# Gated heads: the place of one weight tile's rounding, and where the next stage's first products stand on TensorE

## The chip, the cores and the metric

One core of one Trainium2 chip runs the whole program. The metric is device time in microseconds (us), from runs of the kernel before and of the changed one. PE is TensorE (matrix products), PEld its weight loads, DVE is VectorE, ACT is ScalarE, POOL is GpSimd, and SP is SyncE, which here only issues DMAs.

## What is computed

The program computes two blocks of a network over 768 tokens (256 of context and 512 of a grid) with a width of 1024. The change touches one stage of the second block: the eight gated heads. Cut to what matters:

```python
f, k = lb + (1 - lb) * sigmoid(f_raw), 1 - f        # both directions
gcum = cumsum(log f) within a chunk of 128 tokens
att  = einsum('bhtd,bhtsd,bhsd->bhts', q, exp(gcum_t - gcum_s), k)
o    = einsum('bhts,bhsv->bhtv', att, v) + einsum('bhtd,bhdv->bhtv', q * exp(gcum), s)
s    = exp(glast) * s + einsum('bhsd,bhsv->bhdv', k * exp(glast - gcum), v)
o    = rms_norm(o_forward + o_backward) * silu(gate)
```

Here `f_raw` (for the forward and the backward direction), `q`, `v` and `gate` are projections of the tokens with columns of the matrix `w_in`. The stage after it, the grouped state-space stage, needs `dt`, a further 64 columns of `w_in`, and projections of its own.

## The kernel before

**Projections.** `gated_heads` walks over 41 weight tiles: for each head h five of them, FF and FB (`f_raw` of the two directions), Q, V and G (the gate), in this order, and then one tile for `dt`. A weight tile is 128 x 1024 in float32. It arrives by a DMA from SP into one of two slots of `ring`. ACT rounds it to its high part (`high(n)`, a CAST, L3119), DVE subtracts to get the low part (`low(n)`, L3273), both into `ring_twin`, and SP loads the tile after the next into the slot once the low part is made. PE then makes three products for each of eight slices of the width: L366, L367 and L368, in `product3`. Eight slices make a lot: 24 matmuls of 128 x 384 for half of all tokens (FF, FB and V have two lots each), or 24 of 128 x 512 for the grid's tokens alone (Q and G). One slice of a lot, three matmuls, is a unit here. Lots go by turns into banks 6 and 7 of PSUM, and ACT copies each out (`evict`, L3125).

**A head.** The order on each engine is written out by hand. Every head runs through 14 places, `at` = 1 to 14. On PE, `fill(FILL[at - 1])` puts so many units of the projection behind the head's own work at each place, 64 units or eight lots in all. The projection runs nine lots ahead of the head: during head h PE projects the second half of FF of head h + 1 up to the first half of FF of head h + 2. That last lot begins in the fill of place 12 and is the first to use the tile `n + 5 + FF`. In the last head only one lot, eight units, is left, and it is used up at places 1 and 2.

**Levels.** The decays between two tokens of a chunk are made on seven levels. For each, POOL takes differences of cumulated logs (L2970, L2971, into `hg_dec`, two buffers), ACT exponentiates (`near`, L3194), DVE multiplies by keys and queries (`mixed`, L3317 and L3318, into `hg_mix`), PE multiplies (`products(lv)`, L3039), and DVE puts the result into `hg_att` (`kept`, L3327 and L3330). Products of levels 0 to 7 stand at the head's start and at places 1 to 7. Beside them stand the transposes of v (L3074, place 1), of the weighted keys (`key_rows`, L3054, places 2 and 5), the state updates (`updates`, L3064, places 3 and 6; DVE's `states`, L3339) and at place 10 the head's output (L3090, L3093), eight matmuls of attention and sixteen of states in the trace's count of two passes each.

**The end of a head.** ACT makes the decays of the next head at place 12 (`decays`, L3155 to L3159, for the directions 0 and 1), which DVE weights by the keys at place 13 (`weighted`, L3307 and L3309), and DVE makes the next head's first `mixed` at place 14. DVE's `pre` (L3350) and `tail` (L3356), PE's `squares` (L3045) and ACT's `rstd` (L3169, L3170) normalise a head's output.

**The last head and the next stage.** `leading()` makes the next stage's first two lots (16 units) inside this one, with `lead(count)`; they stay in banks 6 and 7, and the next stage copies them out. In the last head `dt` is transposed through PSUM at place 7 (L3100) and copied out by ACT (L3232, `dt_kept`), and DVE and ACT work on it at places 9 to 11. A stage ends with a barrier of all engines; the next stage's first evictions are L3702.

Of the kernel before, what the change touches and what calls it, by code (L numbers as in the profile page):

```python
# [14 lines left out]
P = 128  # L15
# [4 lines left out]
NC = T // P  # L20
# [2868 lines left out]
def gated_heads(core, k, hT, lower, norm_w, oT, dt, loga, par, ready, base, onward):  # L2889
# [4 lines left out]
    nc, d, ps = core.nc, core.dram, k.ps  # L2894
    H, LV, DEC = HG_HEADS, LEVELS, 2
    PART = (((0, 384), (384, 384)), ((NCTX, NX),))
    with ExitStack() as ctx:
# [16 lines left out]
        dT, dT2, dt_tmp = v[0:64, :], f[0:64, 0, :], f[:, 1, 0:64 * NC].rearrange("p (c a) -> p c a", c=NC)  # L2914
        dt_rows, loga_rows = (a.rearrange("p c a h -> p c (a h)") for a in (dt, loga))
# [8 lines left out]
        FF, FB, Q, V, G = range(5)  # L2924
# [16 lines left out]
        with core.stage("w_in*2", "const_in", "high_ready", "low_ready", "lot_done", "evicted", "sig_ready", "f_ready",  # L2941
# [38 lines left out]
            def _(pe):  # L2980
# [21 lines left out]
                def leading():  # L3002

                    for a, (n, t0, nt) in enumerate(((0, 0, 384), (0, 384, 384))):
                        at = ring_at(len(tiles) + n)
                        pe.wait_ge(low_ready, len(tiles) + n + 1)
                        pe.wait_ge(evicted, len(lots) - 1 + a)
                        if a == 0:
                            pe.wait_ge(dt_kept, 1)
                        for j in range(KD):  # L3010
                            c = slice(P * j, P * j + P)
                            mm = product3(pe, ps[:, 6 + a, 0:nt], (wh[:, at, c], wl[:, at, c]),
                                          (hT[0][:, j, t0:t0 + nt], hT[1][:, j, t0:t0 + nt]), j == 0, j == KD - 1)
                            if j == KD - 1:
                                mm.then_inc(lot_done, 1)
                            yield
                leads = leading()

                def lead(count):
                    for _ in range(count):  # L3020
                        next(leads, None)

                fill(72)
                for h in range(H):
                    p = h % 2

                    def products(lv):
                        a = att_of(h, lv)
                        if a >= 2:
                            pe.wait_ge(att_kept, a - 1)  # L3030
                        if lv == 0:
                            pe.wait_ge(q_ready, h + 1)
                        else:
                            pe.wait_ge(mix_ready, level_of(h, lv))
                        for c in range(NXC):
                            t = slice(P * c, P * c + P)
                            keys, queries = (ks[:, t], q[:, p, t]) if lv == 0 else (mix[:, level_of(h, lv) % 2, 0, t],
                                                                                 mix[:, level_of(h, lv) % 2, 1, t])
                            mm = pe.matmul(ps[:, a % 2, t], keys, queries, start=True, stop=True)  # L3039
                        mm.then_inc(att_done, 1)  # L3040

                    def squares(h):
                        pe.wait_ge(sq_ready, h + 1)
                        pe.wait_ge(pre_ready, h + 1)
                        pe.matmul(ps[:, 5, :], k.ones[:], scr[:], start=True, stop=True).then_inc(ss_done, 1)  # L3045
# [20 lines left out]

                    products(0)
                    for at in range(1, 2 * LV + 1):
                        if at <= LV:
                            products(at)  # L3070
                        if at == 1:
                            pe.wait_ge(evicted, lot_of(h, V, 1) + 1)
                            for c in range(NC):
                                mm = pe.transpose(turn(c), v[:, P * c:P * c + P], k.ident[:])  # L3074
                                if c in (3, NC - 1):
                                    mm.then_inc(vt_done, 1)
                        if at == 2:
                            key_rows(0)
                        if at == 3:
                            updates(0)  # L3080
                        if at == 5:
                            key_rows(1)
                        if at == 6:
                            updates(1)
                        if at == 10:
                            pe.wait_ge(att_kept, (h + 1) * (LV + 1))
                            pe.wait_ge(S_ready, 2 * h + 2)
                            for c in range(NXC):
                                o = ps[:, 5, P * c:P * c + P]
                                pe.matmul(o, vt[:, C0 + c, :], att[:, c, :], start=True, stop=False)  # L3090
                                for dr in range(2):
                                    slot = ORDER[dr][C0:].index(C0 + c)
                                    mm = pe.matmul(o, S[:, dr, slot, :], qe[:, p, dr, P * c:P * c + P], start=False, stop=(dr == 1))  # L3093
                            mm.then_inc(o_done, 1)
                        if at == 2 and h > 0:
                            squares(h - 1)
                        if at == 7 and h + 1 == H:
                            pe.wait_ge(dt_turned, 2)
                            for c in range(NC):
                                mm = pe.transpose(ps[:, 6, 64 * c:64 * c + 64], dT2[:, P * c:P * c + P], k.ident[0:64, 0:64])  # L3100
                            mm.then_inc(dt_done, 1)
                        fill(FILL[at - 1])
                        if h + 1 == H and at > 8:
                            lead((3, 3, 3, 3, 2, 2)[at - 9])
                squares(H - 1)

            @block.scalar
            def _(act):
# [88 lines left out]
                for h in range(H):  # L3197
                    m, n, last = 8 * (h + 1), 5 * (h + 1), h + 1 == H
                    for at in range(1, 2 * LV + 1):
# [29 lines left out]
                        if at == 8:  # L3229
                            if last:  # L3230
                                act.wait_ge(dt_done, 1)
                                act.copy(dt_rows, ps[:, 6, 0:64 * NC].rearrange("p (c a) -> p c a", c=NC)).then_inc(dt_kept, 1)  # L3232
                            act.preload_act_table_set("sigmoid_and_others")
                            if not last:
                                forget(h + 1)
# [17 lines left out]
                            squares(h)  # L3253
                        if at == 12 and not last:
                            decays(h + 1, 0)
                            decays(h + 1, 1)
                            evict(m + 6)
                        if at == 13 and not last:
                            high(n + 5 + FF)
                            near(h + 1, 1)  # L3260
                rstd(H - 1)

# [1 line left out]
            def _(dve):  # L3264
# [105 lines left out]
                for h in range(H):  # L3370
                    n, last = 5 * (h + 1), h + 1 == H
                    for at in range(1, 2 * LV + 1):
# [41 lines left out]
                        if at == 12:  # L3414
                            pre(h)
                        if at == 13 and not last:
                            weighted(h + 1, 0)
                            low(n + 5 + FF)
                        if at == 14 and not last:
                            mixed(h + 1, 1)  # L3420
                        if at == 5 and h > 0:
# [773 lines left out]
```

## Time and profile before

| | |
|---|---|
| time of the kernel, median of 3 | 3500.74 us (3500.51 to 3502.58) |
| the profiled execution | 3506.6 us, span 3504.8 us |
| PE busy | 3281.6 us, 94% |
| DVE busy | 2541.5 us, 73% |
| ACT busy | 1616.3 us, 46% |
| POOL busy | 546.7 us, 16% |
| granted clock of PE, mean | 0.969 |

The gated heads' stage runs from about 846 us to 1324 us of the span. The profiler's execution is one of its own; its rows add up to 3504.8 us, and a difference made from them is carried over to the median. The granted clock of PE has two levels, 2.4 GHz (1.0 in the rows) and 1.2 GHz (0.5); a stretch with a value between them has some of each.

### The profile page before, as it was taken

The numbers are of one execution on the slowest core, as the hardware profiler recorded it, in microseconds if no ns is written. First come the engines' busy times: TensorE is split into PE (matmuls) and PEld (weight loads), VectorE is DVE, ScalarE is ACT, GpSimd is POOL, SyncE is SP. The second block draws the span as 40 slices with busy tenths as digits, with TensorE's granted clock in tenths as the row PEclk, the third lists the DMA queues.
The fourth block names the chain that finished last, engine by engine and source line by source line (L and its number), as shares of the span: only waits on it lengthen the run. The fifth ranks groups of instructions, "written<-read, shape, count | busy, mean of one in ns | idle before, by whom it ended". The sixth has DMA issues, their size and how long they took to land. (4 is left out here: it accounts for less than half of the span.)

```text
span 3504.8 us, 48242 instructions
## 1 busy us (share of the span) xinstructions
PE 3281.6 (94%) x18404; PEld 2863.2 (82%) x18404; DVE 2541.5 (73%) x4368; ACT 1616.3 (46%) x2671; POOL 546.7 (16%) x357
## 2 busy tenths in 40 slices
PE   7997998997999999999998997999997999999997
PEld 3886997775898888888876885999886888999996
DVE  2656886254788786888884444899995887888886
ACT  4433432324555554676664323333663444444444
POOL 0211000000324330000000000455000111222220
PEclk9998999998999999999999999999998999999999
DMA  5101110342111102111113234344468998999994
GB/s 218 44 25 55 31 37 19 114 175 90 49 49 49 49 31 62 55 55 61 55 55 131 91 139 175 117 144 141 156 216 305 352 356 332 351 358 350 347 358 151
DMA packets 152468, 521.20 MB, mean 149 GB/s; under 512 B 19136, under 2 KB 66096, under 8 KB 132400
## 3 DMA queue, kind: packets, MB, share of 16 engines
q1 hardware_dynamic: 133808, 383.90, 30.9%
q0 software_dynamic: 18432, 134.23, 10.2%
q8 instruction: 147, 2.41, 0.3%
q14 instruction: 81, 0.66, 0.1%
HBM read 474.01 MB, written 44.06 MB: 148 GB/s over the span
## 5 line engine op out<-in xcount | busy, mean ns | idle before, releaser
L366 PE MATMUL ps<-hT_high,ring_twin 128*128 128x384 f32 (+1 forms) x1768 | 691.2, 391 | 55.6 <-DVE ring_twin L3273 33.1
L368 PE MATMUL ps<-hT_high,ring_twin 128*128 128x384 f32 (+1 forms) x1768 | 646.2, 366 | 0.0
L367 PE MATMUL ps<-hT_low,ring_twin 128*128 128x384 f32 (+1 forms) x1696 | 617.9, 364 | 0.0
L366 PEld LDWEIGHTS ps<-hT_high,ring_twin 128*128 128x128 f32 x1768 | 341.5, 193 | 106.4 <-DVE ring_twin L3273 38.6
L368 PEld LDWEIGHTS ps<-hT_high,ring_twin 128*128 128x128 f32 x1768 | 340.1, 192 | 31.5
L367 PEld LDWEIGHTS ps<-hT_low,ring_twin 128*128 128x128 f32 x1696 | 328.4, 194 | 30.1 <-issue 4.3
L366 PE MATMUL ps<-ex_vh,ex_al 128*128 128x512 f32 x768 | 301.0, 392 | 21.7 <-DVE ex_al L2812 21.7
L2331 POOL TENSOR_TENSOR pr_wl<-pr_w,pr_wh 128x1024 fp32r<-128x1024 f32 x58 | 147.1, 2538 | 1005.3 <-ACT pr_wh L2390 1005.3
L368 PE MATMUL ps<-ex_vh,ex_ah 128*128 128x512 f32 x768 | 301.5, 393 | 0.0
L367 PE MATMUL ps<-ex_vl,ex_ah 128*128 128x512 f32 x768 | 301.4, 392 | 0.0
L2667 POOL DMA_INDIRECT ex_uv<-in_peer_uv,rows_at x128 | 168.6, 1317 | 810.8 <-DVE ex_acc L2771 570.6
L2722 ACT CAST ex_vh<-ex_v 128x1024 fp32r<-128x1024 f32 x128 | 134.1, 1048 | 163.8 <-PE ps L368 135.3
L2807 DVE TENSOR_TENSOR ex_vl<-ex_v,ex_vh 128x1024 fp32r<-128x1024 f32 x128 | 156.4, 1222 | 54.8 <-ACT ex_vh L2722 54.8
L366 PEld LDWEIGHTS ps<-ex_vh,ex_al 128*128 128x128 f32 x768 | 145.3, 189 | 52.4 <-DVE ex_vl L2807 16.4
L368 PE MATMUL ps<-ex_xh,ex_uh 128*128 128x384 f32 x512 | 171.9, 336 | 0.0
L366 PE MATMUL ps<-ex_xh,ex_ul 128*128 128x384 f32 x512 | 171.7, 335 | 0.0
L367 PE MATMUL ps<-ex_xl,ex_uh 128*128 128x384 f32 x512 | 171.5, 335 | 0.0
L368 PEld LDWEIGHTS ps<-ex_vh,ex_ah 128*128 128x128 f32 x768 | 145.0, 189 | 30.5
L367 PEld LDWEIGHTS ps<-ex_vl,ex_ah 128*128 128x128 f32 x768 | 145.2, 189 | 29.1
L2771 DVE SCALAR_TENSOR_TENSOR ex_acc<-ex_uv,ex_wts,ex_acc 128x1024 f32<-128x1024 f32 x127 | 162.6, 1280 | 4.1 <-DVE ex_acc L2771 0.5
L366 PE MATMUL ps<-ex_xh,pr_wl 128*128 128x384 f32 (+1 forms) x464 | 162.9, 351 | 1.1 <-POOL pr_wl L2331 1.1
L368 PE MATMUL ps<-ex_xh,pr_wh 128*128 128x384 f32 (+1 forms) x464 | 162.3, 350 | 0.0
(610 smaller groups left out, 7604.4 us busy)
## 6 DMA issues: line engine op xcount, KB each, us to landing
ex_v<-in_peer_uv SPq DMA_DIRECT2D x128, 512.0 KB, 7.0
pr_w<-in_peer_u SPq DMA_DIRECT2D x64, 512.0 KB, 3.8
ex_u<-in_peer_u SPq DMA_DIRECT2D x64, 512.0 KB, 7.9
ring<-in_w_in_ma SPq DMA_DIRECT2D x48, 512.0 KB, 3.3
gates_by_expert<-sg_gbuf SPq DMA_DIRECT2D x6, 4096.0 KB, 15.0
ex_g<-gates_by_expert SPq DMA_DIRECT2D x32, 768.0 KB, 8.2
ring<-in_w_in_hg SPq DMA_DIRECT2D x40, 512.0 KB, 3.3
ring<-in_w_merge SPq DMA_DIRECT2D x36, 512.0 KB, 3.7
```

The lines of the kernel that those rows point to most:

```text
L366: pe.matmul(out, a[1], b[0], start=start, stop=False)
L367: pe.matmul(out, a[0], b[1], start=False, stop=False)
L368: return pe.matmul(out, a[0], b[0], start=False, stop=stop)
L2331: pool.tensor_tensor(wl[:, n % R, :], w[:, n % W, :], wh[:, n % R, :].bitcast(F32), ALU.subtract).then_inc(low_ready, 1)
L2667: pool.indirect_dma_start(uv[:, n % UV, :], None, d["peer_uv"], bass.IndirectOffsetOnAxis(ap=rows_at[:, n:n + 1], axis=0)).then_inc(uv_in[ ...
L2722: act.copy(vh[:, m % R, :], v[:, m % R, :]).then_inc(vh_ready, 1)
L2771: dve.scalar_tensor_tensor(out=acc[:], in0=uv[:, n % UV, D:2 * D], scalar=wts[:, n:n + 1], in1=acc[:], op0=ALU.mult, op1=ALU.add).then_inc ...
L2807: dve.tensor_tensor(vl[:, m % R, :], v[:, m % R, :], vh[:, m % R, :].bitcast(F32), ALU.subtract).then_inc(vl_ready, 1)
```

## The change

It has four parts. First, in heads 0 to 6, the CAST of the tile `n + 5 + FF` on ACT moves from the start of place 13 to place 12, between the decays of the two directions, and its subtraction on DVE moves at place 13 ahead of `weighted(h + 1, 0)`. Second, on PE the transposes of v at place 1 move ahead of `products(1)`, in all heads. Third, the `dt` transposes go to bank 5 in place of bank 6 and wait for `rstd` of the head before, so that the leading lots no longer wait for `dt_kept`; the last head's output at place 10, which also uses bank 5, waits for it instead. Fourth, the 16 units of `lead` move from places 9 to 14 (3, 3, 3, 3, 2, 2) to places 3 to 10 (2, 1, 2, 1, 2, 1, 1, 3), with the last 3 behind the last `squares`.

```diff
@@ leading
                         pe.wait_ge(evicted, len(lots) - 1 + a)
-                        if a == 0:
-                            pe.wait_ge(dt_kept, 1)
@@ tensor
                     for at in range(1, 2 * LV + 1):
-                        if at <= LV:
-                            products(at)
                         if at == 1:
                             pe.wait_ge(evicted, lot_of(h, V, 1) + 1)
                             for c in range(NC):
                                 mm = pe.transpose(turn(c), v[:, P * c:P * c + P], k.ident[:])
                                 if c in (3, NC - 1):
                                     mm.then_inc(vt_done, 1)
+                        if at <= LV:
+                            products(at)
...
                         if at == 10:
                             pe.wait_ge(att_kept, (h + 1) * (LV + 1))
                             pe.wait_ge(S_ready, 2 * h + 2)
+                            if h + 1 == H:
+                                pe.wait_ge(dt_kept, 1)
...
                         if at == 7 and h + 1 == H:
                             pe.wait_ge(dt_turned, 2)
+                            pe.wait_ge(rstd_ready, h)
                             for c in range(NC):
-                                mm = pe.transpose(ps[:, 6, 64 * c:64 * c + 64], dT2[:, P * c:P * c + P], k.ident[0:64, 0:64])
+                                mm = pe.transpose(ps[:, 5, 64 * c:64 * c + 64], dT2[:, P * c:P * c + P], k.ident[0:64, 0:64])
                             mm.then_inc(dt_done, 1)
                         fill(FILL[at - 1])
-                        if h + 1 == H and at > 8:
-                            lead((3, 3, 3, 3, 2, 2)[at - 9])
+                        if h + 1 == H:
+                            lead((0, 0, 2, 1, 2, 1, 2, 1, 1, 3, 0, 0, 0, 0)[at - 1])
                 squares(H - 1)
+                lead(3)
@@ scalar
-                                act.copy(dt_rows, ps[:, 6, 0:64 * NC].rearrange("p (c a) -> p c a", c=NC)).then_inc(dt_kept, 1)
+                                act.copy(dt_rows, ps[:, 5, 0:64 * NC].rearrange("p (c a) -> p c a", c=NC)).then_inc(dt_kept, 1)
...
                         if at == 12 and not last:
                             decays(h + 1, 0)
+                            high(n + 5 + FF)
                             decays(h + 1, 1)
                             evict(m + 6)
                         if at == 13 and not last:
-                            high(n + 5 + FF)
                             near(h + 1, 1)
@@ vector
                         if at == 13 and not last:
+                            low(n + 5 + FF)
                             weighted(h + 1, 0)
-                            low(n + 5 + FF)
```

ACT's order from the first decays to the first level's exponential, in the first full head before the change (the CAST of `ring` is `high`):

```order
L3155 ACTIVATE hg_ebl<-hg_cum 128x6
L3157 ACTIVATE hg_qe<-hg_cum 128x512
L3159 ACTIVATE hg_kd<-hg_kd 128x768
L3125 COPY hg_v<-ps 128x384
L3119 CAST ring_twin_50<-ring 128x1024
L3194 ACTIVATE hg_dec<-hg_dec 128x1024 x2
```

And the same stretch of ACT after the change, from the last instruction of the first direction's decays on:

```order
L3161 ACTIVATE hg_kd<-hg_kd 128x768
L3121 CAST ring_twin_50<-ring 128x1024
L3157 ACTIVATE hg_ebl<-hg_cum 128x6
L3159 ACTIVATE hg_qe<-hg_cum 128x512
L3161 ACTIVATE hg_kd<-hg_kd 128x768
L3127 COPY hg_v<-ps 128x384
L3196 ACTIVATE hg_dec<-hg_dec 128x1024 x2
```

The CAST has moved past three activations and one copy; nothing else of ACT's order changes in these heads.

DVE's order at the same place before the change, from the head's `pre` (`oT`) to the next head's first `mixed`:

```order
L3350 SCALAR_TENSOR_TENSOR oT<-ps,hg_norm_w,hg_gate 128x512
L3307 TENSOR_TENSOR hg_kd<-hg_kd,hg_k 128x768
L3309 TENSOR_TENSOR hg_qe<-hg_qe,hg_q 128x512
L3273 TENSOR_TENSOR ring_twin_50<-ring,ring_twin_50 128x1024
L3317 TENSOR_TENSOR hg_mix<-hg_dec,hg_k 128x512
L3318 TENSOR_TENSOR hg_mix<-hg_dec,hg_q 128x512
```

DVE's order there after the change:

```order
L3352 SCALAR_TENSOR_TENSOR oT<-ps,hg_norm_w,hg_gate 128x512
L3275 TENSOR_TENSOR ring_twin_50<-ring,ring_twin_50 128x1024
L3309 TENSOR_TENSOR hg_kd<-hg_kd,hg_k 128x768
L3311 TENSOR_TENSOR hg_qe<-hg_qe,hg_q 128x512
L3319 TENSOR_TENSOR hg_mix<-hg_dec,hg_k 128x512
L3320 TENSOR_TENSOR hg_mix<-hg_dec,hg_q 128x512
```

The subtraction stands two instructions earlier; what comes before and behind the three is the same.

PE's order in the last head before the change, from the products of level 3 to the first leading unit (L366; `hg_f` is `dt` here):

```order
L3039 MATMUL ps<-hg_mix 128x128 x4
L3064 MATMUL ps<-hg_vt,hg_ktok 128x128 x5
L3039 MATMUL ps<-hg_mix 128x128 x8
L3054 MATMUL ps<-ident,hg_kd 128x128 x6
L3039 MATMUL ps<-hg_mix 128x128 x4
L3064 MATMUL ps<-hg_vt,hg_ktok 128x128 x5
L3039 MATMUL ps<-hg_mix 128x128 x4
L3100 MATMUL ps<-ident,hg_f 128x64 x6
L366 MATMUL ps<-hT_high,ring_twin_50 128x384
```

PE's order there after the change, from the end of the unit before level 4 to the first unit behind the second transposes of keys:

```order
L368 MATMUL ps<-hT_high,ring_twin_50 128x384
L3037 MATMUL ps<-hg_mix 128x128 x4
L366 MATMUL ps<-hT_high,ring_twin_50 128x384
L367 MATMUL ps<-hT_low,ring_twin_50 128x384
L368 MATMUL ps<-hT_high,ring_twin_50 128x384
L3037 MATMUL ps<-hg_mix 128x128 x4
L3052 MATMUL ps<-ident,hg_kd 128x128 x6
L366 MATMUL ps<-hT_high,ring_twin_50 128x384
```

Levels 4 and 5, which stood back to back (x8), now have a leading unit between them, and each later place has one or two, up to place 10.

## Rows read from the trace of the kernel before

**Rows 1.** The page: PE's busy time (us, share of the span, instructions).

```profile
PE 3281.6 (94%) x18404; PEld 2863.2 (82%) x18404; DVE 2541.5 (73%) x4368; ACT 1616.3 (46%) x2671; POOL 546.7 (16%) x357
```

**Rows 2.** PE's waits, 940 to 1290 us: total us, times, longest us.

```profile
PE ps L366 <- DVE ring_twin L3273: 15.2, 7, 2.2
```

**Rows 3.** Windows from wait to wait: stretch, us, each engine's busy us, PE clock.

```profile
1002.53:1057.59 55.06, 52.90 (x321) 49.91 (x321) 43.86 (x57) 31.09 (x44) 19.56 (x15) 0.97 0.15 49
1112.63:1166.11 53.48, 51.33 (x321) 48.34 (x321) 43.87 (x57) 31.08 (x44) 19.57 (x15) 1.00 0.15 50
```

**Rows 4.** Timeline of PE up to one such wait: start us, us, instruction, [idle before].

```profile
994.72 0.39 PE L366 MATMUL ps<-hT_high,ring_twin 128*128 128x512 f32 x1
...
999.97 0.39 PE L368 MATMUL ps<-hT_high,ring_twin 128*128 128x512 f32 x1
1002.53 0.44 PE L366 MATMUL ps<-hT_high,ring_twin 128*128 128x384 f32 x1 [2.17 <-DVE ring_twin L3273]
```

**Rows 5.** Timeline of DVE, 996 to 1010 us.

```profile
997.81 1.19 DVE L3307 TENSOR_TENSOR hg_kd<-hg_kd,hg_k 128x768 f32<-128x768 f32 x1
998.92 1.57 DVE L3309 TENSOR_TENSOR hg_qe<-hg_qe,hg_q 128x512 f32<-128x512 f32 x1
1000.42 2.06 DVE L3273 TENSOR_TENSOR ring_twin<-ring,ring_twin 128x1024 fp32r<-128x1024 f32 x1
...
1004.00 0.68 DVE L3318 TENSOR_TENSOR hg_mix<-hg_dec,hg_q 128x512 f32<-128x512 f32 x1
```

**Rows 6.** Timeline of ACT, 993 to 1005 us.

```profile
994.60 0.85 ACT L3159 ACTIVATE hg_kd<-hg_kd 128x768 f32<-128x768 f32 x1 [0.26 <-DVE hg_kd L3300]
...
997.26 0.85 ACT L3159 ACTIVATE hg_kd<-hg_kd 128x768 f32<-128x768 f32 x1 [0.26 <-DVE hg_kd L3300]
...
998.38 1.05 ACT L3119 CAST ring_twin<-ring 128x1024 fp32r<-128x1024 f32 x1
```

**Rows 7.** Timeline of SP, 975 to 1000 us.

```profile
983.57 8.69 SPq L2958 DMA_DIRECT2D ring<-in_w_in_hg  x2
```

**Rows 8.** The page: DMA issues by line, KB each, us to landing.

```profile
ring<-in_w_in_hg SPq DMA_DIRECT2D x40, 512.0 KB, 3.3
```

**Rows 9.** Timeline of DVE ahead of head 0, 889.5 to 899 us.

```profile
890.53 2.11 DVE L3273 TENSOR_TENSOR ring_twin<-ring,ring_twin 128x1024 fp32r<-128x1024 f32 x1
892.56 1.84 DVE L3307 TENSOR_TENSOR hg_kd<-hg_kd,hg_k 128x768 f32<-128x768 f32 x1
...
897.37 0.68 DVE L3318 TENSOR_TENSOR hg_mix<-hg_dec,hg_q 128x512 f32<-128x512 f32 x1
```

**Rows 10.** Timeline of PE at the start of the next head.

```profile
1008.39 1.05 PE L3039 MATMUL ps<-hg_q,hg_sg 128*128 128x128 f32 x8
...
1010.17 0.82 PE L3074 MATMUL ps<-ident,hg_v 128*128 128x128 f32 x6
1010.74 0.42 PE L366 MATMUL ps<-hT_high,ring_twin 128*128 128x384 f32 x1
```

**Rows 11.** PE's waits, 1290 to 1330 us, the last head and behind it.

```profile
PE ps L3039 <- DVE hg_mix L3318: 5.8, 3, 2.4
PE ps L366 <- ACT ma_raw L3702: 4.3, 1, 4.3
```

**Rows 12.** Windows over the last head's middle and the next stage's first lot.

```profile
1293.20:1310.00 16.80, 10.36 (x58) 9.56 (x58) 14.76 (x26) 6.38 (x9) 5.13 (x4) 0.70 0.00 1
...
1325.87:1332.60 6.73, 6.73 (x27) 6.73 (x27) 0.60 (x7) 1.29 (x2) 0.00 (x0) 0.63 0.65 164
```

**Rows 13.** Timeline of PE, end of the last head.

```profile
1313.69 0.42 PE L366 MATMUL ps<-hT_high,ring_twin 128*128 128x384 f32 x1
...
1320.54 1.02 PE L3045 MATMUL ps<-hg_scr,ones 128*128 128x512 f32 x2
```

**Rows 14.** Timeline of DVE, end of the last head.

```profile
1314.82 0.74 DVE L3350 SCALAR_TENSOR_TENSOR oT<-ps,hg_norm_w,hg_gate 128x512 f32<-128x512 f32 x1
1322.98 0.69 DVE L3356 TENSOR_TENSOR oT<-oT,hg_scr 128x512 f32<-128x512 f32 x1 [7.42 <-ACT hg_scr L3170]
```

## Prediction

> **What bounds the kernel now.** I began with the page: PE is busy for 94% of the span [rows 1], so in this stage a gain must come from PE's own idle time or from its clock. Next I asked who PE waits for in the heads. From 940 to 1290 us there is one line only: seven waits, 15.2 us together, all for DVE's low part of a weight tile [rows 2]. They are the seven uses of the tile `n + 5 + FF`, one in each of heads 0 to 6. Then I cut the stage from one wait to the next. A head takes 55.06 us at a mean clock of 0.97, but one of them, which has the same wait and as many instructions, takes 53.48 us at 1.00 [rows 3]. So a wait costs twice: PE stands for 2.17 us, and in six of the seven heads the clock goes to its lower level for a moment behind it, which costs 55.06 - 53.48 = 1.58 us more.
>
> The timelines say why the tile is late. PE issues its last product of lot G at 999.97 and is free for the next about 0.23 us later (products of 512 columns follow each other at that distance), at 1000.2. It starts at 1002.53 [rows 4], right behind the end of the subtraction, 1000.42 + 2.06 = 1002.48 [rows 5]. DVE has by then done two operations that nobody needs before the next head. ACT's CAST runs from 998.38 to 999.43 [rows 6], so in the old order not even ACT was early enough: both halves of the move are needed.
>
> **Part 1, the tile's rounding.** *ACT.* The first direction's decays end at 994.60 + 0.85 = 995.45, and the second's last activation starts at 997.26, when DVE releases it [rows 6]. Between stand two short activations (0.8 us in all), which fit behind a CAST from 995.45 to 996.50: they end at 997.3. So the 1.05 us go into time in which ACT waited, and the second decays are late by 0.05 us or nothing. The CAST itself needs two things. Its slot must be free, which is so when the last lot of V is done, at 994.7, where lot G starts [rows 4]. Its data must have landed: issued at 983.57 [rows 7], plus 3.3 us [rows 8], is 987. Neither makes it wait. *DVE.* The subtraction now starts where `weighted` started, 997.81 [rows 5], 1.3 us after the CAST. It takes 2.06 us there and 2.11 us at most [rows 5, 9], POOL being at work beside it each time, so it is done by 999.92, and PE wants it at 1000.2. The margin is 0.3 us by the worst row and 1.2 us if it took only what `weighted`'s first operation took there, 1.19 us. I take the wait as wholly gone: 15.2 us.
>
> The Trainium skill bears on this margin ("SBUF — State Buffer", section "SBUF: two separate sides"): VectorE with two SBUF inputs and GpSimd share a port pair that is locked for a whole instruction, and the loser blocks. The rows agree so far that the same subtraction takes 2.06 to 2.11 us beside POOL. By the rule DVE would lose at most the rest of one POOL instruction, so the sum would be the same, and only the chance of a late tile smaller.
>
> *The clock.* With the wait gone I expect the lower clock behind it gone too: 6 x 1.58 = 9.5 us. The trace's one head at 1.00 shows that it is no fixed part of a head; it does not show that the waits cause it, since that head had its wait as well. The Trainium skill ("TensorE: Matmul & The Clock Gate", section "HAM oscillation") puts the loss at the throttled time multiplied by one half. With the clock of 0.97 in 55.06 us the shortfall is 1.65 us a head and the sum 9.9 us instead of 9.5 us, which changes nothing that I conclude.
>
> *What is late next.* PE arrives at the next head 2.17 + 1.58 = 3.75 us earlier against DVE, so 1008.39 becomes 1004.6 [rows 10]. `products(0)` reads old data. `products(1)` needs DVE's `mixed`, which ended at 1004.00 + 0.68 = 1004.68 [rows 5]; in the new order the same five operations run in the same stretch. The opening, ahead of head 0, already has the new order there: 890.53 to 898.05, 7.52 us [rows 9], against 997.81 to 1004.68, 6.87 us. So `mixed` ends between 1004.7 and 1005.3.
>
> **Part 2, transposes first.** Products 0 and 1 take 1010.17 - 1008.39 = 1.78 us together, 0.89 us each, and the transposes 1010.74 - 1010.17 = 0.57 us [rows 10]. `products(1)` would be due at 1004.6 + 0.9 = 1005.5 in the old order, 0.2 us behind the worst case, and 1006.1 in the new. It moves no work and is worth nothing by itself; it makes the cover thicker. ACT gets v's transposes 0.9 us earlier, DVE the products of level 1 0.6 us later, and neither was waited for by PE. The sum of part 1 is 15.2 + 9.5 = 24.7 us.
>
> **Parts 3 and 4, the last head.** Here PE has no projection left behind place 2 and waits three times for `mixed`, 5.8 us [rows 11], with a clock of 0.70 in the 16.8 us around it [rows 12]: 0.30 x 16.8 = 5 us of full speed are missing there. A unit is (1320.54 - 1313.69) / 13 = 0.53 us [rows 13]. Ten units stand now at places 3 to 9, 5.3 us, almost the size of the waits that they fill. Some of them sit in front of `products` or `updates` and would delay the chain that DVE walks, yet PE works more evenly, which should give back part of the clock. Most of what the clock costs there lies in or beside waits, so I count an eighth to a half of the 5 us for the moment at which the head's output can start, 0.6 to 2.5 us, and take 1.5 us. The bound on the bad side is 5.3 us later, if no unit fell into a wait.
>
> Behind the output there were 13 units, from 1313.69 to 1320.54, and only then `squares`, `rstd` and `tail` (to 1322.98 + 0.69 = 1323.67 [rows 14]). `pre`, which `squares` needs, had long been ready. Now three units end at 1315.3 by that clock, and `squares` starts at 1314.82 + 0.74 = 1315.56 rather than 1320.54: 5.0 us less. The `dt` work on ACT and DVE that stands ahead of `pre` doesn't start earlier than the output does, so I take 4.6; at the lower clock three units take 3.2 us, `squares` 0.9 us more, and 3.0 are left. The last three units, 1.6 us, run beside `rstd` and `tail`, which end 1323.67 - 1320.54 = 3.1 us behind the start of `squares`.
>
> PE then waits 4.3 us [rows 11] at the stage's border, and the next stage's first lot runs at 0.63 for 6.7 us [rows 12], which is 2.5 us lost. With the last units nearer to the border the wait is shorter (about 2.8 us) and the clock may be lower for less long: 0.6 us, between 0 and 1.7. The last head and its border give 1.5 + 4.6 + 0.6 = 6.7 us, between 3.6 and 9.3 (0.6 + 3.0 + 0 and 2.5 + 5.0 + 1.7).
>
> **The sum.** 24.7 + 6.7 = 31.4 us. The profiled span would be 3504.8 - 31.4 = 3473.4 us. That execution took 3506.6 us, 5.9 us more than the runs' median; nothing that I remove hangs on that difference, so I take the 31.4 us from the median, 3500.74: 3469.3 us. Everything behind the stage starts by so much earlier, behind a barrier. The likeliest case's own range is 3466 to 3473 us.
>
> **The rivals.** *Half of it comes back.* The tile is just late after all, or `products(1)` waits for `mixed`, or the low clock of each head has another cause and stays. For: margins of 0.3 to 1.2 us in a trace whose same operation varies from 1.19 to 2.11, and a clock that fell in six heads of seven without a proof of the cause. Against: the opening's worst rows still fit. With the clock unchanged the sum is 31.4 - 9.5 = 22 us, 3479 us; with a wait of 1 us left in each of seven heads, clock included, about 17 us, 3484 us.
>
> *The last head gives nothing.* The units delay the chain of levels by the full 5.3 us and eat what the end gives. Then only the 24.7 us are left, 3476 us. For: in that stretch PE is in line ahead of DVE. Against: 5.8 us of waiting that they can fill.
>
> *No change.* The wait goes on one step, from the tile to `products(1)`, at its old size. That needs `mixed` to end about 3 us later than the worst row; no row speaks for it. 3500 us.
>
> *Slower.* DVE and POOL lock each other out for longer in the new order. If the run from the subtraction to `mixed` took twice its 6.87 us, `mixed` would end at 1011.5, and `products(1)`, which began at 1008.39 + 0.89 = 1009.3, would begin 2.2 us later than before in each of seven heads: 3501 + 15 - 7 = 3509 us. It decides from a slip of 4.6 us on, where 1009.3 is passed. The opening, in the same order, shows 0.65 us.
>
> **How the numbers follow.** Full gain in heads and last head 0.70; heads full and the last head nothing 0.09; half comes back 0.14; no change 0.04; slower 0.03. A measurement of this kernel can tell about 0.2%, 7 us, from no change. All of the first three are beyond that: faster 0.93, the same 0.04, slower 0.03. The range must leave out no more than 0.2: it goes down to 3462 (9.3 us in the last head is 3467, and 0.7 us less in each head beyond that) and up to 3480, which takes in the last head without gain and the unchanged clock.
>
> **What would show it.** In the changed kernel's profile the waits of PE for the low part of a tile between 940 and 1290 us are gone, the windows of one head are 53.48 - 2.17 = 51.3 us at a clock of 1.00, and PE does not wait for `hg_mix` at a head's start. The subtraction ends before 1000 in that head's time. In the last head units stand between the levels, `squares` follows the output within 2 us or so, and the wait at the border is nearer to 3 than to 4.3 us. I am wrong if the windows stay near 53 us, if the clock of a head stays at 0.97 without a wait, or if a new line of waits for `hg_mix` holds what the tile's line held.

## The result and the profile after

The changed kernel takes 3467.47 us (median of 4 runs, 3466.3 to 3470.02) against 3501.49 us (3500.51 to 3502.58): a ratio of 0.9904, interval 0.9887 to 0.9921, or 34 us less, between 28 and 40. The forecast was 31.4 us less, 3469.3 us. The two profiled executions differ by more, 3504.8 against 3464.5 us; of these 40.3 us 6.0 lie ahead of the stage, in code that no part touches, so the parts are priced below from windows of the stage itself.

The waits of PE first. The view of waits from 895 to 1255 us, heads 0 to 6, has no line left where [rows 2] had seven waits. In the last head and behind it, 1255 to 1292 us (who waits for whom: total us, times, longest):

```profile
PE ps L3037 <- DVE hg_mix L3320: 3.0, 3, 1.9
PE ps L366 <- ACT ma_raw L3704: 2.7, 1, 2.7
PE ps L3043 <- DVE oT L3352: 0.3, 1, 0.3
```

The first two answer to 5.8 and 4.3 us in [rows 11]. Before the change the same view had one more line, for the copy of `dt` out of bank 6, which is gone:

```profile
PE ps L366 <- ACT rows L3232: 0.7, 1, 0.7
```

The wait for `ma_raw` stands at the border to the next stage. Windows of the changed kernel, the first from one head's `products(0)` to the next, the second from the last head's `products(0)` to the next stage's first lot, the third that lot:

```profile
994.74:1045.81 51.07, 51.07 (x321) 48.42 (x321) 45.05 (x57) 31.07 (x46) 20.91 (x14) 1.00 0.16 53
...
1250.05:1287.81 37.76, 31.70 (x209) 28.81 (x209) 30.93 (x53) 20.67 (x31) 13.85 (x10) 0.95 0.02 3
1287.81:1293.60 5.79, 5.79 (x24) 5.79 (x25) 0.57 (x6) 1.26 (x2) 0.00 (x0) 0.71 0.75 191
```

The same three cuts before the change (the first is one of the six heads with the low clock, cut at `products(0)` too):

```profile
953.33:1008.39 55.06, 52.89 (x322) 49.90 (x322) 43.86 (x56) 31.08 (x44) 19.56 (x14) 0.97 0.14 49
```

```profile
1282.05:1325.87 43.82, 33.08 (x209) 30.88 (x209) 29.54 (x52) 19.93 (x29) 10.21 (x8) 0.86 0.02 2
1325.87:1332.40 6.53, 6.53 (x24) 6.53 (x25) 0.58 (x6) 1.23 (x2) 0.00 (x0) 0.62 0.67 169
```

In such a line stand the stretch, its length, the busy time of PE, PEld, DVE, ACT and POOL, PE's clock, the DMA share and GB/s. In a head PE is now busy for every microsecond, 51.07 of 51.07, at the full clock of 2.4 GHz. Over heads 0 to 6 the windows add up to 356.58 us against 382.94: 26.4 us less. The last head gives 43.82 - 37.76 = 6.1 us, the next stage's first lot 0.7 us. Together 33.2 us; the rest of the 34 is within the spread of the runs.

The timeline of DVE after the change, which answers to [rows 5]:

```profile
1039.22 1.46 DVE L3275 TENSOR_TENSOR ring_twin<-ring,ring_twin 128x1024 fp32r<-128x1024 f32 x1
1040.60 1.84 DVE L3309 TENSOR_TENSOR hg_kd<-hg_kd,hg_k 128x768 f32<-128x768 f32 x1
...
1045.41 0.69 DVE L3320 TENSOR_TENSOR hg_mix<-hg_dec,hg_q 128x512 f32<-128x512 f32 x1
```

And of ACT, which answers to [rows 6]:

```profile
1036.76 1.03 ACT L3121 CAST ring_twin<-ring 128x1024 fp32r<-128x1024 f32 x1
...
1038.67 0.85 ACT L3161 ACTIVATE hg_kd<-hg_kd 128x768 f32<-128x768 f32 x1 [0.24 <-DVE hg_kd L3302]
```

The last activation of the second direction still waits for DVE (0.24 us, 0.26 before), so the CAST cost ACT nothing. The five operations of DVE take 1046.10 - 1039.22 = 6.88 us, against 6.87 before. PE at that head's start:

```profile
1045.81 1.05 PE L3037 MATMUL ps<-hg_q,hg_sg 128*128 128x128 f32 x8
1046.70 0.82 PE L3070 MATMUL ps<-ident,hg_v 128*128 128x128 f32 x6
1047.36 1.06 PE L3037 MATMUL ps<-hg_mix 128*128 128x128 f32 x8
```

`mixed` is done at 1046.10. `products(1)` starts at 1047.36; without the transposes ahead of it it would have been due at 1046.70, still 0.6 us behind `mixed`. And the end of the last head, PE and then DVE, which answer to [rows 13] and [rows 14]:

```profile
1277.61 0.39 PE L3090 MATMUL ps<-hg_att,hg_vt 128*128 128x128 f32 x2
...
1282.40 1.10 PE L3043 MATMUL ps<-hg_scr,ones 128*128 128x512 f32 x2 [0.34 <-DVE oT L3352]
1287.81 0.61 PE L366 MATMUL ps<-hT_high,ring_twin 128*128 128x384 f32 x1 [2.75 <-ACT ma_raw L3704]
```

```profile
1281.51 0.74 DVE L3352 SCALAR_TENSOR_TENSOR oT<-ps,hg_norm_w,hg_gate 128x512 f32<-128x512 f32 x1
1284.92 0.69 DVE L3358 TENSOR_TENSOR oT<-oT,hg_scr 128x512 f32<-128x512 f32 x1 [2.67 <-ACT hg_scr L3172]
```

### The profile page after: what moved, and what is told of

Its sections match the earlier page's. It is cut to its first block and busy times, and to the rows that moved or that the text cites. A ratio compares the mean times of both kernels' runs of the same rounds, so it can differ in the third digit from the quotient of the medians.

```text
span 3464.5 us, 48243 instructions
## 1 busy us (share of the span) xinstructions
PE 3265.2 (94%) x18404; PEld 2847.0 (82%) x18404; DVE 2550.3 (74%) x4368; ACT 1616.3 (47%) x2671; POOL 557.2 (16%) x357
## 3 DMA queue, kind: packets, MB, share of 16 engines
q1 hardware_dynamic: 133808, 383.90, 31.1%
## 5 line engine op out<-in xcount | busy, mean ns | idle before, releaser
L366 PE MATMUL ps<-hT_high,ring_twin 128*128 128x384 f32 (+1 forms) x1768 | 687.1, 389 | 38.2 <-DVE ring_twin L3275 17.6
L366 PEld LDWEIGHTS ps<-hT_high,ring_twin 128*128 128x128 f32 x1768 | 338.3, 191 | 86.2 <-DVE ring_twin L3275 20.2
L366 PE MATMUL ps<-ex_vh,ex_al 128*128 128x512 f32 x768 | 301.4, 392 | 20.3 <-DVE ex_al L2812 20.3
L366 PEld LDWEIGHTS ps<-ex_vh,ex_al 128*128 128x128 f32 x768 | 145.4, 189 | 50.7 <-DVE ex_vl L2807 16.0
L366 PE MATMUL ps<-ex_xh,ex_ul 128*128 128x384 f32 x512 | 171.7, 335 | 0.0
L2970 POOL TENSOR_TENSOR hg_dec<-hg_cum 128x512 f32<-128x512 f32 x56 | 78.0, 1393 | 549.9 <-DVE hg_cum L3299 496.3
L366 PE MATMUL ps<-ex_xh,pr_wl 128*128 128x384 f32 (+1 forms) x464 | 162.9, 351 | 1.1 <-POOL pr_wl L2331 1.1
## 6 DMA issues: line engine op xcount, KB each, us to landing
gates_by_expert<-sg_gbuf SPq DMA_DIRECT2D x6, 4096.0 KB, 15.2
```

The source lines that it names most:

```text
L366: pe.matmul(out, a[1], b[0], start=start, stop=False)
L2970: pool.tensor_tensor(ke, crossed(cums[:, h % 2], size, False, True), crossed(cums[:, h % 2], size, False, False), ALU.subtract)
```

## The experiments

Theory A is the prediction's: the tile's wait and the low clock behind it are one cost, and both go with part 1. Against it stood B (the transposes' new place carries part of the gain) and C (the low clock has a cause of its own). The table has, from each kernel's windows, the sum of the seven stretches between `products(0)` of one head and of the next, and the stretch from the last head's `products(0)` to the next stage's first lot; single executions, whose heads repeat within 0.1 us. The first of the seven stretches is shorter (54.22 us before, 50.22 after) and stands in the sum alone.

| kernel | heads 0 to 6, us | one head, us | last head to border, us |
|---|---|---|---|
| before | 382.94 | 55.06, one 53.47 | 43.82 |
| changed | 356.58 | 51.06 | 37.76 |
| round_alone | 356.64 | 51.06 | 45.05 |
| no_round | 382.93 | 55.05, one 53.48 | 38.77 |
| cast_alone | 382.87 | 55.05, one 53.46 | 38.80 |
| sub_alone | 365.39 | 52.32 | 38.78 |
| products_first | 356.61 | 51.06 | 37.98 |
| busy_wait | 373.45 | 53.47 | 43.56 |
| units_late | 356.64 | 51.07 | 44.55 |
| units_behind | 356.64 | 51.07 | 43.04 |
| units_in_waits | 356.54 | 51.05 | 39.03 |

### round_alone: part 1 alone

```diff
@@ the kernel before
                             decays(h + 1, 0)
+                            high(n + 5 + FF)
                             decays(h + 1, 1)
...
-                            high(n + 5 + FF)
...
+                            low(n + 5 + FF)
                             weighted(h + 1, 0)
-                            low(n + 5 + FF)
```

> The kernel before with part 1 alone: the CAST between the decays and the subtraction ahead of the weighted keys. Theory A (the tile's wait and the low clock behind it are one cost, 7 x 2.4 us and 6 x 1.6 us): the heads take 26 us less, 51.1 us each at a clock of 1.00, and the last head and the border stay at 43.8 us. Theory B (a good part of the gain comes from the transposes ahead of products(1), which cover a late mixed): PE waits for hg_mix in each head, 0.2 to 1 us, and the gain is 18 to 24 us.

3475.21 us against 3502.19, ratio 0.9923 (0.9907 to 0.994). The heads take 26.3 us less, and PE waits for nothing in them. Part 1 alone makes the whole gain of the heads; B falls. The last head became 1.2 us longer than before, which I had not expected. It is the clock: from the fourth level on `mixed` ends at the same time behind `products(0)` as before, within 0.02 us, but from the products of place 6 to the transposes of `dt` PE takes 5.81 us at a clock of 0.50, where it took 4.71 us at 0.63 for the same work.

### no_round: parts 2 to 4 alone

The changed kernel with the three lines of the diff above undone.

> The changed kernel with part 1 undone: transposes first, dt in bank 5 and the spread units are left. Theory A: heads stay at 55.05 us with a wait of 2.17 us each, and only the last head and the border gain, 6 to 7 us in all against before. Theory B: the heads gain a little as well, so that more than 8 us come out.

3495.69 us against 3502.19, ratio 0.9981 (0.9971 to 0.9992). Heads as before, last head 5.1 us shorter and the next stage's first lot 0.7 us: A, though 5.8 us is a little under the 6 to 7 expected. In the runs the two halves of the change add up, 27.0 + 6.5 = 33.5 us against 34. The windows are sharper: up to the border round_alone has 25.1 us less than before, no_round 5.1 us and the changed kernel 32.4 us, 2.3 us more than both together. Parts 2 to 4 also take back what part 1 loses in the last head.

### busy_wait: products in place of the wait

```diff
@@ the kernel before, projection()
                     for n, (_, parts, _) in enumerate(tiles):
+                        if n % 5 == 0 and n > 5:
+                            for _ in range(10):
+                                pe.matmul(ps[:, 4, :], hT[0][:, 0, 0:P], hT[0][:, 0, NCTX:T], start=True, stop=True)
                         pe.wait_ge(low_ready, n + 1)
```

> The kernel before, with ten extra products of 128 x 512 (about 2.2 us) into a bank that nobody reads, in front of each of the seven waits for the tile; they change no output. The head's schedule is as before, but PE computes instead of standing. Theory A (standing still is what lowers the clock): every head takes 53.5 us at 1.00, about 9.5 us less than before in all, although PE has more work. Theory C (the low clock has another cause, a regular one): heads stay at 55.05 us at 0.97, no gain, or even a loss.

3493.01 us against 3502.19, ratio 0.9971 (0.996 to 0.9983). Two windows of this kernel:

```profile
948.37:1001.84 53.47, 53.47 (x332) 50.20 (x331) 43.84 (x56) 31.09 (x44) 19.59 (x15) 1.00 0.15 50
1001.84:1055.31 53.47, 53.47 (x331) 50.22 (x331) 43.86 (x56) 31.08 (x44) 19.56 (x15) 1.00 0.15 50
```

Against the window 953.33 to 1008.39 above this head has ten more products on PE, the same 31.1 us of ACT, and is 1.6 us shorter, with the clock at 1.00 in all seven. The sum is 9.5 us less, the very sum that the prediction had for the clock. So it is standing still at that place that brings the lower clock; C falls. The kernel is faster with 70 useless products than without them. It also parts the two costs: 9.5 us of clock, and 373.45 - 356.58 = 16.9 us of waiting. (The ten products fill the wait and no more: they start at 995.24 and the tile's first product at 997.56, 2.3 us later, and the head is as long as the one fast head before the change, 53.47 us.)

### cast_alone and sub_alone: half of part 1

cast_alone is the changed kernel with `low(n + 5 + FF)` behind `weighted(h + 1, 0)` again; sub_alone is the changed kernel with `high(n + 5 + FF)` at place 13 again.

> The changed kernel with DVE's half of part 1 undone: the CAST is early, the subtraction stands behind the weighted keys again. Theory A: the subtraction starts at the same place as before, PE waits 2.2 us in each head, the clock falls again, heads at 55.0 us: only the 6 to 7 us of the last head are left. The rival, that ACT's late CAST was the real limit: heads near 51 us.

> The changed kernel with ACT's half of part 1 undone: the CAST is late again (ends 3.4 us behind the start of the second direction's activation), the subtraction stands ahead of the weighted keys and DVE waits for it, at 999.5 in the old head's time. Theory A: the subtraction ends near 1001.0, PE waits about 1 us (0.7 to 1.6) in each head, the clock falls in fewer heads or none, and mixed of the next head is late by some 1.6 us, so that PE waits a second time at products(1): heads 52 to 53.5 us. The rival, that the DVE's order alone was enough: heads near 51.1 us.

One execution each: 3498.06 and 3476.18 us. The early CAST without the early subtraction gives nothing in the heads (382.87). The early subtraction without the CAST gives two thirds: 365.39, with these waits of PE and these windows:

```profile
PE ps L366 <- DVE ring_twin L3275: 7.1, 7, 1.0
```

```profile
999.65:1051.97 52.32, 51.31 (x321) 48.32 (x321) 42.95 (x56) 30.98 (x44) 19.39 (x15) 1.00 0.15 51
1051.97:1104.31 52.34, 51.33 (x322) 48.34 (x322) 42.96 (x56) 30.98 (x44) 19.39 (x15) 1.00 0.15 51
```

PE stands for 1.0 us in each head and the clock stays at 1.00 in all seven. A second wait at `products(1)`, which I expected, does not come. The timeline of DVE here:

```profile
1045.77 1.86 DVE L3275 TENSOR_TENSOR ring_twin<-ring,ring_twin 128x1024 fp32r<-128x1024 f32 x1 [1.56 <-ACT ring_twin L3121]
...
1049.26 0.68 DVE L3311 TENSOR_TENSOR hg_qe<-hg_qe,hg_q 128x512 f32<-128x512 f32 x1
...
1050.62 0.68 DVE L3320 TENSOR_TENSOR hg_mix<-hg_dec,hg_q 128x512 f32<-128x512 f32 x1
```

DVE stands for 1.56 us for the CAST. Yet `mixed` ends only 0.3 us later behind the start of `pre` than in the changed kernel (7.85 against 7.54 us), because the five operations now take 5.53 us in place of 6.88: POOL's two pairs are over at 1048.53, and the operations behind that run alone (L3311 takes 0.68 us, 1.52 in the changed kernel). PE itself arrives more than 1 us later, so nothing waits. I had counted neither. ACT's half of the move is worth 365.39 - 356.58 = 8.8 us, 1.26 us in each head.

### products_first: part 2 undone

The changed kernel with `products(at)` ahead of the transposes at place 1.

> The changed kernel with the transposes of v behind products(1) again. Theory A: worth nothing by itself, as mixed ends 0.6 us ahead of where products(1) would then start: heads 51.05 us, no wait for hg_mix. Theory B: PE waits for hg_mix at each head's start, heads 51.2 us or more.

3466.15 us in one execution; 356.61 us in the heads, no wait in them. Part 2 is worth nothing there, as forecast, and 0.2 us in the last head (37.98 against 37.76, one execution each).

### units_late and units_behind: where the last head's gain is

```diff
@@ units_late, the changed kernel
-                            lead((0, 0, 2, 1, 2, 1, 2, 1, 1, 3, 0, 0, 0, 0)[at - 1])
+                            lead((0, 0, 0, 0, 0, 0, 0, 0, 3, 3, 3, 3, 2, 2)[at - 1])
                 squares(H - 1)
-                lead(3)
@@ units_behind, the changed kernel
-                            lead((0, 0, 2, 1, 2, 1, 2, 1, 1, 3, 0, 0, 0, 0)[at - 1])
+                            lead((0, 0, 0, 0, 0, 0, 0, 0, 3, 3, 0, 0, 0, 0)[at - 1])
                 squares(H - 1)
-                lead(3)
+                lead(10)
```

> The changed kernel with the sixteen leading units back at places 9 to 14 (3, 3, 3, 3, 2, 2) and dt still in bank 5. Theory A (the order of the units is worth nearly all of the last head's gain, the bank only the 0.7 us wait for dt_kept): from the output to squares 9.4 us as before, from the last head's products(0) to the border 43 to 45 us against 37.8. The rival (the bank is worth more, as PE stood at the copy of dt): 41 us or less.

> The changed kernel with no unit between the levels: three units at place 9, three at 10, and ten behind the last squares. Theory A (two gains add up: squares not behind the units, and seven units inside waits that PE has anyway): output to squares 4.8 us as in the changed kernel, but the border 3 to 4 us later behind squares, since seven more units of 0.53 us stand there and only some lie beside rstd and tail. The output itself starts at 28 to 30 us behind products(0), because PE stands between the levels and its clock falls. The rival (the units between the levels were free of charge and of use, all the gain is in squares): the same time to the border as the changed kernel within 1 us.

One execution each, 3472.44 and 3476.88 us. The border comes 44.55 and 43.04 us behind `products(0)`, against 37.76. In pieces, us:

| kernel | `products(0)` to output | output to `squares` | `squares` to border |
|---|---|---|---|
| before | 29.05 | 9.44 | 5.33 |
| units_late | 29.68 | 9.55 | 5.33 |
| units_behind | 29.68 | 4.86 | 8.50 |
| changed | 27.56 | 4.79 | 5.41 |

To put `squares` ahead of ten units makes it 4.7 us earlier, but the units then stand between it and the border, and 1.5 us is left. To have seven of them between the levels instead of behind `squares` is worth 5.3 us, with `squares` already early; what it is worth with `squares` late no run shows. For units_late the rival with the bank fell (44.55 us, not 41 or less): against round_alone, 45.05 us, the other bank and the transposes' place give 0.5 us together. The windows of the last head, units_late and then units_behind:

```profile
1251.45:1296.00 44.55, 33.82 (x209) 31.27 (x209) 30.87 (x53) 20.55 (x31) 13.84 (x10) 0.88 0.02 2
```

```profile
1253.83:1296.87 43.04, 34.15 (x209) 31.33 (x209) 30.86 (x53) 20.56 (x31) 13.85 (x10) 0.88 0.02 3
```

As many PE instructions as in the changed kernel (x209), more busy time (33.8 and 34.2 against 31.7 us) and a clock of 0.88 against 0.95. Of the 5.3 us between units_behind and the changed kernel, 2.45 are the same products done at a better clock and 2.8 are time in which PE no longer stands: the units in the waits are no load, and they keep the clock up.

### units_in_waits: more units in the largest wait

```diff
@@ the changed kernel
-                            lead((0, 0, 2, 1, 2, 1, 2, 1, 1, 3, 0, 0, 0, 0)[at - 1])
+                            lead((0, 0, 2, 4, 2, 1, 1, 0, 0, 3, 0, 0, 0, 0)[at - 1])
```

> The changed kernel with the 13 units of the last head at places 3 to 10 as 2, 4, 2, 1, 1, 0, 0, 3 instead of 2, 1, 2, 1, 2, 1, 1, 3: three units more in the largest wait left (1.89 us, place 5), none in front of the output. Theory A (the output waits for PE, not for states): it starts up to 1.1 us earlier, the low clock of 3.4 us goes as well; 1 to 2 us less. The rival (the output starts when DVE's states are done, which were 0.2 us ahead of it): under 0.4 us less, no difference to be measured.

Ratio to the kernel before 0.9913 (0.9893 to 0.9932) by three runs, 3468.92 to 3472.13 us, not to be told from the changed kernel's; the fourth took 8753.55 us, which nothing here explains. The wait at place 5 shrank from 1.89 to 0.33 us, but the one at place 6 grew from 0.51 to 2.05 us, and the three together are 3.0 us as before. The output still starts 27.5 us behind `products(0)`, now behind a wait for the states (timeline of PE):

```profile
1278.55 0.59 PE L3101 MATMUL ps<-ident,hg_f 64*128 64x64 f32 x6
1281.19 0.69 PE L3090 MATMUL ps<-hg_att,hg_vt 128*128 128x128 f32 x2 [1.34 <-DVE hg_S L3341]
1281.67 1.06 PE L3093 MATMUL ps<-hg_qe,hg_S 128*128 128x128 f32 x4
```

Four of the state products take 1.06 us at the output's start, against 0.61 us at the full clock: the low clock moved from a place where PE had time onto the output. The border is 1.3 us later (39.03), but the next stage's first lot behind it runs at the full clock and takes 1.5 us less than in the changed kernel (4.24 against 5.79 us), so that both have the same time to the lot's end, 43.3 and 43.6 us:

```profile
1292.71:1296.95 4.24, 4.24 (x24) 4.24 (x25) 0.58 (x6) 0.24 (x1) 0.00 (x0) 1.00 0.93 244
```

The rival held: DVE's states, not PE, set the output's start.

### opening_early, after_again, opening_again: a version beyond the change

```diff
@@ the changed kernel, DVE
-                scan(0, 0)
-                scan(0, 1)
                 low(5)
+                scan(0, 0)
+                scan(0, 1)
                 weighted(0, 0)
```

> The changed kernel with the subtraction of the sixth tile ahead of the two scans in the opening, where DVE stood idle for 3.2 us; PE waits 5.74 us for it now, with the low clock for 6.8 us behind it. Theory A: the wait for the tile is gone, but products(1) of head 0 then waits 2 to 3 us for mixed, since the chain log, scan, decays, mixed is what limits it; 4 to 6 us less than the changed kernel. The rival (the chain is the only bound, PE's wait just moves): under 2 us less.

> The changed kernel once more, beside the next one on the same chip. From the stage's first product to the next stage's cumulated sums I expect 450.8 us as in its first profile, and 3467 to 3468 us in all.

> The kernel with the sixth tile's subtraction ahead of the scans once more, beside the changed kernel on the same chip. Theory A: the 3.8 us that the stage was shorter in its profile are real and reach the end, 3463 to 3465 us, 3 to 4 us less than the changed kernel. The rival: the stages behind give them back or the difference is lost in the spread of runs, under 2 us.

Before head 0 PE waits 5.74 us for the sixth tile, in the changed kernel too, and the clock is at 0.50 for 5 us behind it (not 6.8, as the first expectation says). With its subtraction early the wait moves (PE's waits, 860 to 900 us, first try):

```profile
PE ps L3037 <- DVE hg_mix L3320: 4.2, 1, 4.2
```

The first try took 3467.7 us, ratio 0.9902 (0.9886 to 0.9919). On one chip, opening_again took 3467.85 us (0.9901, 0.9885 to 0.9918) and after_again 3468.3 us (0.991, 0.9893 to 0.9926): no difference. Both expectations, 4 to 6 and 3 to 4 us less, were missed, though four runs each, spread over 5 and 6 us, can't exclude a gain of that size either.

In the profiles the stage, up to the next stage's sums over `loga` (L3573), is 3.8 and 3.9 us shorter. Only 2.3 us of that are won in the opening. The other 1.6 us are the first lot behind the border, 4.2 us at the full clock in place of 5.8, and units_in_waits has that too, with the opening as it was. PE's waits from 1289 to 1345 us in opening_again:

```profile
PE ps L366 <- ACT ma_raw L3704: 4.0, 2, 2.7
PE ps L3564 <- ACT ma_xtok L3740: 2.2, 1, 2.2
PE ps L366 <- DVE ring_twin L3862: 0.7, 1, 0.7
```

after_again has only the first line's 2.7 and the second line. In opening_again PE waits 1.3 us more for evicted lots and 0.7 us for a tile (units_in_waits, with the same fast first lot, 0.3 and 0.7 us). From those sums to the products of `ma_b` (L3629), some 40 us, the two kernels of this section take 2.8 and 2.5 us more than the changed one. From the sums to the end of the span opening_again took 2174.6 us and after_again 2170.7; in the first pair it was 2175.0 and 2170.9. In the other ten profiles, with the same code there, it is between 2167.6 and 2172.4 us. So the loss of the first 40 us is shown twice, and where the rest goes, or whether it is more than the spread, stays open.

## Why the prediction was right

**The bound and the wait.** Right. All seven waits went and PE is never idle in a head. The term was a little too small: 15.2 us in the rows, 16.9 us measured by busy_wait against the changed kernel. A pause costs about 0.24 us more than the idle time in its row, in sub_alone too, where rows of 1.0 us cost 1.26 us each. The row counts from the modelled end of the product before, 999.97 + 0.39 = 1000.36, while the next could have started at 1000.20, and the first product behind the pause keeps the next one off for 0.28 us in place of 0.17 (1002.53 to 1002.81).

**The clock.** Right in size and, by busy_wait, in cause: 9.5 us forecast, 9.5 measured. The sum for the heads was 24.7 us, the windows give 26.4.

**ACT's cover.** Right: the CAST ran from 1036.76 to 1037.79, and the second decays ended when DVE let them. Both halves of the move were needed for the full gain, but not alike: DVE's alone gives 17.5 us, ACT's alone nothing.

**DVE's margin.** The subtraction took 1.46 us in its new place, not 2.06 to 2.11, and `weighted`'s first operation took 1.84 in place of 1.19. The sum of the five stayed, 6.87 and 6.88 us, while their shares changed. It is no constant: in the opening it is 7.52 us, and 5.53 us in sub_alone, where POOL ends earlier. The tile was done at 1040.68, about 0.9 us ahead of PE.

**The transposes.** Worth nothing by themselves, as forecast; the worst case that they were to cover (`mixed` up to 0.65 us late) did not come.

**The last head.** The three terms were 1.5, 4.6 and 0.6 us. From `products(0)` to the output it is 29.05 us before and 27.56 after, 1.5 less; from there to `squares` 9.44 and 4.79, 4.7 less; the first lot 0.7 less. The numbers are right, the reasons only in part, and that all three fit so well is in part luck.

The first term is a balance. Up to the output, parts 2 to 4 alone give 0.5 us (no_round, 28.57), part 1 alone costs 1.2 us (round_alone, 30.28), and with part 1 in place the others give 2.7 us, more than the 2.5 that the prediction held for the most. It had no term for what part 1 does to the last head. The bad bound of 5.3 us later was far off.

The second term is right for `squares`, but that is not yet time at the border: units_behind has `squares` just as early and gains 1.5 us by it. The rest needs the seven units to find room between the levels. The prediction had them there, as units that nearly fill the waits, but priced only the case in which none fell into one.

The third term's reason is not confirmed. The wait at the border shrank as forecast, from 4.3 to 2.75 us, but only because three units stand in what was the wait: from `squares` to the border it is 5.33 us before and 5.41 after. And the first lot, up to the sums over `loga`, is as short without the shorter wait: 5.65 us in round_alone and 5.77 in units_late, both with a wait of 4.31 us, against 5.81 after and 6.53 before. What sets the clock of that lot stays open.

**The sum.** 31.4 forecast, 33.2 in the windows, 34 measured. None of the rivals occurred. Three side sums of the prediction are off, and none of them moves the forecast: 2.5 + 5.0 + 1.7 is 9.2, not 9.3; the low bound of the second term comes out at 1320.54 - (1313.69 + 3.2) - 0.9 = 2.7 us by its own numbers, not 3.0; and a wait of 1 us left in each head, with the clock unchanged, gives 31.4 - 7 - 9.5 = 14.9 us, not 17. What that rival would really have cost sub_alone shows: 8.8 us of the heads' gain, as the clock stays up behind pauses of 1 us.

## What to carry to other kernels

When PE stands for a tile's low part, look at where both halves of its rounding stand in their engines' orders: here the operations ahead of it were needed by no one before the next head, and ACT had a gap of its length. Price such a wait with the clock behind it, from two windows of the same work at either clock; and a wait that can't be removed is worth filling with work that is due later anyway. A gain of a few microseconds ahead of a barrier should be followed past it: of the 2.3 us won in the opening none could be measured at the end, and the next stage began with more waits for evictions and a tile.

## What the runs showed of the hardware

Seven pauses of 2.17 us brought the lower clock six times in each of three kernels (before, no_round, cast_alone), once not; seven pauses of 1.0 us (sub_alone) never did. Where the low clock falls is not fixed by the pause alone: behind the same 2.75 us at the border the first lot runs at 0.71 in the changed kernel and at 1.00 in units_in_waits and opening_again, and round_alone's last head, with the code and nearly the waits of before, is 1.2 us longer. The Trainium skill ("TensorE: Matmul & The Clock Gate", section "HAM oscillation") puts the loss at half of the throttled time. With a clock of 0.97 over 55.06 us that is an estimate of 1.65 us a head, and busy_wait agrees: 55.06 - 53.47 = 1.6 us.
